# A five-layer network on one core: compression weights outside the ring, bias tables in parts, and weight rounding on two engines instead of three

## What is computed

```python
h = h + moba_nsa_mixer(rmsnorm(h), ...)      # "even": 8 heads of attention plus 8 heads that join three attentions by gates
h = h + sqrelu_mlp(rmsnorm(h), w1, w2)       # "mlp0"
h = h + fox_mixer(rmsnorm(h), ...)           # "fox": 16 heads, bias cum[q] - cum[k] from forget gates
h = h + sqrelu_mlp(rmsnorm(h), w1, w2)       # "mlp1"
x = rmsnorm(h, final_norm)
mod = silu(c) @ w_ada + b_ada                # nine vectors: shift, scale and gate three times
h = x + 0.5 * gt1 * swiglu(modulate(rmsnorm(x), sh1, sc1))      # "glu0"
h = h + gt2 * hybrid_mixer(modulate(rmsnorm(h), sh2, sc2))      # "dil": pooled channels and 8 heads
h = h + 0.5 * gt3 * swiglu(modulate(rmsnorm(h), sh3, sc3))      # "glu1"
return rmsnorm(h, g_final)
```

## Time and profile before

| | |
|---|---|
| median of 3 runs (1163.77 to 1170.25) | 1168.05 us |
| the profiled execution | 1166.54 us |
| its span, first to last instruction | 1164.7 us |
| PE, weight loads of PE | 95%, 85% |
| DVE, ACT, POOL | 66%, 48%, 11% |
| mean granted clock of PE | 0.977 |
| DMA | 236.82 MB, mean 203 GB/s |
| unit loads | 177 of 1 MB, median 5.0 us |

### The profile page before, as it was taken

One profiled execution on the slowest core, in us unless ns is written; L12 is line 12 of the kernel. 1 busy time (PEld: TensorE's weight loads), 2 busy tenths in 40 slices (PEclk: granted clock), 3 DMA queues, 4 the chain that ended last, 5 costly groups with the idle time before them and its releaser, 6 DMA issues.

```text
span 1164.7 us, 17629 instructions
## 1 busy us (share of the span) xinstructions
PE 1107.6 (95%) x7206; PEld 993.6 (85%) x7206; DVE 766.8 (66%) x1186; ACT 564.6 (48%) x843; POOL 132.2 (11%) x209
## 2 busy tenths in 40 slices
PE   6769999999999999999999999999979998999997
PEld 5768778999997988899999779999968977999996
DVE  6445666878778666676766867667676667554555
ACT  5534756434346577653433463333436767333342
POOL 2012212101001022210000110000130131000000
PEclk9779999999999999999999989999999999999999
DMA  7532326778784633486767737776754434555551
GB/s 274 222 145 73 109 97 231 276 285 292 281 287 157 249 143 109 155 296 249 244 250 253 288 144 241 267 270 253 243 193 145 145 112 162 193 186 181 181 184 70
DMA packets 39072, 236.82 MB, mean 203 GB/s; under 512 B 4389, under 2 KB 4549, under 8 KB 15952
## 3 DMA queue, kind: packets, MB, share of 16 engines
q1 hardware_dynamic: 26640, 188.76, 44.6%
q0 software_dynamic: 12064, 46.26, 11.7%
q10 hardware_dynamic: 288, 0.68, 0.2%
HBM read 234.58 MB, written 1.10 MB: 202 GB/s over the span
## 4 chain that ended last, share of the span: by engine, by line
PE 84%; DVE 7%; DMA 5%; ACT 2%; issue 1%; SPq 0%; DVEq 0%; ACTq 0%
PE bank L1389 26%; PE bank L1390 26%; PE bank L1391 26%; DMA raw<-in_stream 5%; PE bank L1579 1%; PE bank L1561 1%; PE bank L1473 1%; DVE w_lo L950 1%; PE bank L1550 1%; PE bank L1549 1%; ACT w_hi L629 1%; DVE h L981 1%; DVE w_lo L964 1%; DVE logit L1106 1%; DVE ada_raw L1168 0%
## 5 line engine op out<-in xcount | busy, mean ns | idle before, releaser
L1389 PE MATMUL bank<-a_lo,w_hi 128*128 128x256 f32 x1408 | 406.9, 289 | 6.4 <-ACT pair L851 3.3
L1390 PE MATMUL bank<-a_hi,w_lo 128*128 128x256 f32 x1408 | 402.5, 286 | 0.0
L1391 PE MATMUL bank<-a_hi,w_hi 128*128 128x256 f32 x1408 | 402.4, 286 | 0.0
L964 DVE TENSOR_TENSOR w_lo<-raw,w_hi 128x2048 fp32r<-128x2048 f32 x123 | 280.4, 2290 | 155.3 <-ACT w_hi L643 155.1
L643 ACT ACTIVATE w_hi<-raw 128x2048 fp32r<-128x2048 f32 x123 | 235.4, 1917 | 207.3 <-DMA raw<-in_stream 207.2
L1389 PEld LDWEIGHTS bank<-a_lo,w_hi 128*128 128x128 f32 x1408 | 274.4, 195 | 11.7 <-ACT pair L851 3.5
L1390 PEld LDWEIGHTS bank<-a_hi,w_lo 128*128 128x128 f32 x1408 | 274.5, 195 | 1.8
L1391 PEld LDWEIGHTS bank<-a_hi,w_hi 128*128 128x128 f32 x1408 | 274.1, 195 | 0.0
L1389 PE MATMUL bank<-w_lo,hid_hi 128*128 128x512 f32 x432 | 169.5, 392 | 0.4 <-DVE w_lo L964 0.2
L1390 PE MATMUL bank<-w_hi,hid_lo 128*128 128x512 f32 x432 | 168.9, 391 | 0.0
L1391 PE MATMUL bank<-w_hi,hid_hi 128*128 128x512 f32 x432 | 168.3, 390 | 0.0
(11 more groups left out here) (199 smaller groups left out, 1166.6 us busy)
## 6 DMA issues: line engine op xcount, KB each, us to landing
raw<-in_stream SPq DMA_DIRECT2D x177, 1024.0 KB, 5.0
ada_raw<-in_ada POOLq DMA_DIRECT2D x72, 512.0 KB, 4.8
rel_band<-rel_scratch POOLq DMA_DIRECT2D x1, 2048.0 KB, 15.4
cum_row<-cum_scratch POOLq DMA_DIRECT2D x1, 2048.0 KB, 11.1
h<-in_x SPq DMA_DIRECT2D x2, 512.0 KB, 6.6
raw<-in_stream SPq DMA_DIRECT2D x2, 512.0 KB, 7.7
silu_row<-in_c_row POOLq DMA_DIRECT2D x2, 512.0 KB, 4.3
dil_b<-in_dil_bias POOLq DMA_DIRECT2D x1, 1024.0 KB, 10.5
```

The costliest lines, as they stand in the source:

```text
L964: nc.vector.tensor_tensor(w_lo[:, u % RING, :], raw[:, u % RING, :], w_hi[:, u % RING, :].bitcast(F32), ALU.subtract).then_inc(lo_ready, 2)
L1389: nc.tensor.matmul(dst, l_hi, r_lo, start=start, stop=False)
L1390: nc.tensor.matmul(dst, l_lo, r_hi, start=False, stop=False)
L1391: return nc.tensor.matmul(dst, l_hi, r_hi, start=False, stop=stop)
```

## The change

- The four compression units leave the ring and the list of phases. They lie at the end of the stream and go into `cmpw`, two slots where the modulation rows lie later. SP issues the two of the keys behind units 3 and 5, and the two of the values in front of unit 10, behind a new wait on `cmp_used`. PE multiplies them in `compress`, in four ticks (`CMP_AT`); the later steps of that chain move to earlier ticks; the `cmp` ticks are gone and the heads' list is laid over the ticks that are left.
- `rel_band` comes in two halves, the NSA heads' behind `unit_used` 3, the others' behind 5; `cum_row` in four parts, each behind a unit; VectorE waits for each part at a tick of its own. The forget gates move one tick up. The relative-bias matmul stands behind the first turn.
- GpSimd rounds nothing. In each turn ScalarE and VectorE now round half 0 in the shifted turns too, and half 1 between block 0 and block 1.
- `ada_pieces` of `mlp1` and `glu0` end two J earlier, and the gains one J earlier.
- After the forget gates and in the dil mixer ScalarE does a one-column Exp, which loads that table early. ScalarE scales half of the output rows.

```diff
 PHASES = [
-    ("v_even", 4), ("kcvc", 1), ("kskw", 1), ("nq0", 1), ("cmp0", 1), ("nq1", 1), ("cmp1", 1), ("qm0", 1), ("cmp2", 1), ("km0", 1),
-    ("cmp3", 1), ("km1", 1), ("qm1", 1),
+    ("v_even", 4), ("kcvc", 1), ("kskw", 1), ("nq0", 1), ("nq1", 1), ("qm0", 1), ("km0", 1), ("km1", 1), ("qm1", 1),
...
-POOL_HALVES = sorted([2 * FIRST[_name] + 3 for _name in ("mlp0", "v_fox", "mlp1", "glu0", "uv_dil", "glu1")]
-                     + [2 * FIRST[_name] + 2 for _name in ("glu0", "uv_dil", "glu1")])
+CMP_UNITS = 4
...
+CMP_AT = [("nq0", 0, 1), ("nq1", 0, 0), ("qm0", 0, 0), ("qm0", 0, 1)]
 CT_AT = [("km1", 0, 1), ("km1", 0, 2), ("qm1", 0, 0), ("qm1", 0, 1)]
...
+        cmpw = place("cmpw", [P, 2, UNIT], at=V_at + 2 * D * 4)
...
-            (first, last), j0, n = ADA_OF[name], *((1, FF2 - 1) if name == "glu0" else (2, FF1 - 2))
-            return range(first + (last - first) * (j - j0) // n, first + (last - first) * (j - j0 + 1) // n)
+            (first, last), j0, n = ADA_OF[name], *{"mlp0": (2, FF1 - 2), "mlp1": (2, FF1 - 4), "glu0": (1, FF2 - 3)}[name]
+            return range(first + (last - first) * min(j - j0, n) // n, first + (last - first) * min(j - j0 + 1, n) // n)
...
             for u in range(1, N_UNITS):
                 if u >= RING:
                     sp.wait_ge(unit_used, u - RING + 1)
+                if u == FIRST["qm0"] + 2:
+                    sp.wait_ge(cmp_used, 2)
+                    for half in range(2):
+                        sp.dma_start(cmpw[:, half, :], stream[N_UNITS + 2 + half]).then_inc(cmp_landed[2 + half], 16)
                 sp.dma_start(raw[:, u % RING, :], stream[u]).then_inc(raw_landed[u % RING], 16)
+                if u in (RING - 1, RING + 1):
+                    half = (u - RING + 1) // 2
+                    sp.dma_start(cmpw[:, half, :], stream[N_UNITS + half]).then_inc(cmp_landed[half], 16)
...
-            pool.dma_start(rel_band[:, :, :], bass.AP(rel_dram, 0, [[1, P], [REL + 1, 16], [1, T]])).then_inc(rel_landed, 16)
+            pool.wait_ge(unit_used, 3)
+            pool.dma_start(rel_band[:, HEADS:16, :], bass.AP(rel_dram, HEADS * (REL + 1), [[1, P], [REL + 1, HEADS], [1, T]])).then_inc(rel_landed[0], 16)
+            pool.wait_ge(unit_used, FIRST["kskw"])
+            pool.dma_start(rel_band[:, 0:HEADS, :], bass.AP(rel_dram, 0, [[1, P], [REL + 1, HEADS], [1, T]])).then_inc(rel_landed[1], 16)
...
-            round_second("mlp0")
...
-            pool.dma_start(cum_row[:, :, :], bass.AP(cum_dram, 0, [[0, P], [T, 16], [1, T]])).then_inc(cum_landed, 16)
+            for c in range(4):
+                if c > 0:
+                    pool.wait_ge(unit_used, FIRST["qk_fox"] + c - 1)
+                pool.dma_start(cum_row[:, 4 * c:4 * c + 4, :], bass.AP(cum_dram, 4 * c * T, [[0, P], [T, 4], [1, T]])).then_inc(cum_landed[c], 16)
...
                 for t in range(TT):
                     squares(name, t)
                     if t == 0:
-                        if shift is None:
-                            round_half()
+                        round_half()
                         scale(name)
                     turned(name, t, gain, shift)
+                    if t == 0:
+                        round_half()
...
                     inverse_root(name, 0)
-                if shift is None:
-                    rest_half()
+                rest_half()
                 add(name, sums, gate, 1, 0)
                 turned(name, 0, gain, shift, (0, 1))
                 add(name, sums, gate, 1, 1)
                 turned(name, 0, gain, shift, (2, 3))
+                rest_half()
...
-                        if (name, j) == ("mlp1", FF1 - 1):
+                        if (name, j) == ("mlp1", FF1 - 2):
                             gains(("gf1", "gmix"))
...
-            nc.tensor.matmul(ps[6][0:16, 0:REL], relt[:, :], rpick[:, :], start=True, stop=True).then_inc(rel_rows, 1)
             pe.wait_ge(norms_landed, 16)
             turn_rows("mix0", 0)
+            nc.tensor.matmul(ps[6][0:16, 0:REL], relt[:, :], rpick[:, :], start=True, stop=True).then_inc(rel_rows, 1)
...
+            def compress(v, half):
+
+                pe.wait_ge(blocks_ready, v + 1)
+                pe.wait_ge(cmp_landed[2 * v + half], 16)
+                wr = cmpw[:, half, :].rearrange("p (k c) -> p k c", k=8)
+                for k in range(8):
+                    row_ = HD * (k % 2)
+                    ins = nc.tensor.matmul(ps[(2, 7)[v]][row_:row_ + 30, 0:256], blk[:, v, 8 * half + k, :], wr[:, k, :],
+                                           start=(half == 0 and k < 2), stop=(half == 1 and k >= 6))
+                ins.then_inc(cmp_used, 1)
```

More of the change, by code:

```diff
@@ L320, in build @@
         first_landed = [sem("first_landed0"), sem("first_landed1")]
+        cmp_landed = [sem(f"cmp_landed{i}") for i in range(CMP_UNITS)]
+        cmp_used = sem("cmp_used")
+        rel_landed = [sem("rel_landed0"), sem("rel_landed1")]
+        cum_landed = [sem(f"cum_landed{i}") for i in range(4)]
         hi_ready = sem("hi_ready")
@@ L727, in stack, with pairs @@
                     ins.then_inc(feat_hi, 1)
+            def pairs(v):
+                act.wait_ge(unit_used, FIRST["kcvc"] + 1)
+                for g in range(2):
+                    src = ps[4][HD * g:HD * g + HD, v * T:(v + 1) * T]
+                    nc.scalar.activation(pair[0:HD, v, g, :], src, ACT.Copy)
+                    ins = nc.scalar.activation(pair[HD:P, v, g, 0:T - 1], src[:, 1:T], ACT.Copy)
+                ins.then_inc(pairs_taken, 1)
             def values(kind, which):
@@ L844, in even_extras @@
                     values("even", (3,))
-                if tick.tag == "kskw":
-                    v = tick.part
-                    act.wait_ge(unit_used, FIRST["kcvc"] + 1)
-                    for g in range(2):
-                        src = ps[4][HD * g:HD * g + HD, v * T:(v + 1) * T]
-                        nc.scalar.activation(pair[0:HD, v, g, :], src, ACT.Copy)
-                        ins = nc.scalar.activation(pair[HD:P, v, g, 0:T - 1], src[:, 1:T], ACT.Copy)
-                    ins.then_inc(pairs_taken, 1)
-                for v, where in enumerate((("qm0", 0, 0), ("km1", 0, 0))):
+                for v, where in enumerate((("nq1", 0, 2), ("qm0", 0, 3))):
                     if tick.at(*where):
-                        act.wait_ge(unit_used, FIRST[("cmp1", "cmp3")[v]] + 1)
+                        act.wait_ge(cmp_used, 2 * v + 2)
                         nc.scalar.activation(hid_e[:, v, :], ps[(2, 7)[v]][HD:HD + 30, 0:256], ACT.Copy).then_inc(hidden_half, 1)
-                for v, where in enumerate((("qm0", 0, 2), ("km1", 0, 1))):
+                for v, where in enumerate((("qm0", 0, 0), ("km0", 0, 2))):
                     if tick.at(*where):
@@ L1247, in even_extras @@
             def even_extras(tick):
+                if tick.at("qm1", 0, 0):
+                    dve.wait_ge(rel_landed[1], 16)
                 if tick.at("kcvc", 0, 0):
@@ L1253, in even_extras @@
                     values("even", (2,))
-                if tick.at("nq1", 0, 0):
-                    dve.wait_ge(rel_landed, 16)
+                if tick.at("nq0", 0, 1):
+                    dve.wait_ge(rel_landed[0], 16)
                     nc.vector.memset(pc[:, 0:8, 7:15], BIG)
@@ L1642, in compressed_heads @@
                 ins.then_inc(cpv_done, 1)
+            def compress(v, half):
[7 more added lines that the diff above has]
+                ins.then_inc(cmp_used, 1)
             def even_extras(tick):
-                for v, where in enumerate((("qm0", 0, 2), ("km1", 0, 1))):
+                for c, where in enumerate(CMP_AT):
+                    if tick.at(*where):
+                        compress(c // 2, c % 2)
+                for v, where in enumerate((("nq1", 0, 3), ("km0", 0, 1))):
                     if tick.at(*where):
@@ L1696, in even_unit @@
                     feature_part(u, 4, part, 2)
-                elif tag.startswith("cmp"):
-                    v, half = int(tag[3]) // 2, int(tag[3]) % 2
-                    if half == 0:
-                        pe.wait_ge(blocks_ready, v + 1)
-                    wait_raw(pe, u, 1)
-                    wr = raw[:, u % RING, :].rearrange("p (k c) -> p k c", k=8)
-                    for k in range(8):
-                        row_ = HD * (k % 2)
-                        ins = nc.tensor.matmul(ps[(2, 7)[v]][row_:row_ + 30, 0:256], blk[:, v, 8 * half + k, :], wr[:, k, :],
-                                               start=(half == 0 and k < 2), stop=(half == 1 and k >= 6))
-                    ins.then_inc(unit_used, 1)
                 elif tag == "out_even":
```

113 lines of the change are left out of this document (41 added, 72 removed), and 6 rows, old and new, of the table EVEN_TICKS.

## The result

| | before | after |
|---|---|---|
| median | 1165.91 us (4 runs, 1162.93 to 1170.25) | 1125.16 us (4 runs, 1123.64 to 1126.79) |
| ratio | 1 | 0.9648, 95% interval 0.9609 to 0.9687 |
| profiled execution | 1166.54 us | 1124.25 us |
| its span | 1164.7 us | 1122.4 us |
| PE, DVE, ACT, POOL busy | 95%, 66%, 48%, 11% | 97%, 68%, 51%, 9% |

The change took off 42.3 us of the span where 31.7 were forecast.

What follows compares the result with a forecast made beforehand. TensorE, 95% busy, was taken to lose time to waits and half-clock stretches, mostly from 33 to 182 us. Gains of 25.5 + 1.9 + 3.4 + 0.9 = 31.7 us from 1166.54 gave 1134.8, set at 1135.5 us; range 1126 to 1149.

Steps and rivals of the forecast that it cites:

- The even part: Up to mlp0's first turn: 17.0 us of waits and 10.0 of half clock go, 1.5 comes back; 25.5 us gained.
- Small waits: Even part: new small waits from the moved compression work and loads, taken as 1.5 us, bounds 0 and 6.6.
- The 1.2 us for `pcT`: Even part, at 142 us: this wait stays, with its half-clock stretch costing 3.1 us.
- I leave `gf1` its half-clock stretch: First turn of gf1: its half-clock stretch, priced at 2.5 us, stays because new waits replace the old one.
- the second turns: Six turns: rounding between row blocks makes PE wait, 2.6 us in three plain turns, 6.0 in three with a shift.
- The clean-clock rival: Stretches at 142 and in gf1 go too, 3.1 + 2.5 us, if small waits do not lower the clock: 1130; chance 0.19.
- The load marks: Early loads, signs of being right: kcvc lands in 5 to 7 us, and no long `raw` load before 90 us.
- No `raw` load of more than 8 us before 90: Early loads: a sign of being right, that none before 90 us takes longer than 8 us.
- The fox part: Fox mixer: the logits' wait of 2.2 us goes, the four cum_row loads cost 0.3; 1.9 us gained.
- The turns: Turns: 11.7 us of waits and 1.5 of clock go, less 2.6 + 6.0 + 1.2; 3.4 us gained.
- The 7.9 credited to it: First turn of gmix: modulation two units ahead cuts the wait from 8.5 to some 0.6 us, 7.9 gained.
- Ends: Relative-bias matmul behind the first turn gains 0.2 us, output scalings shared with ScalarE 0.7; 0.9 gained.

Runs made afterwards that it cites:

- a_late_loads: Changed kernel with the loads of units 7 to 14 waiting until one more unit is used; span 1155.0 us.
- a_bias_whole: Changed kernel with the 2 MB bias read in one piece again, as early as in the kernel before; span 1128.9 us.
- a_mod_back: Changed kernel with the modulation's pieces and the two gains back at their old J; span 1130.0 us.
- a_cum_whole: Changed kernel with cum_row read in one 2 MB transfer again; span 1124.1 us.
- a_fox_back: Changed kernel with cum_row in one transfer and the forget gates a tick later, as before; segment mix1 to mlp1 122.11 us.
- probe1: Changed kernel with nine added waits of TensorE in glu1, made by GpSimd memsets; span 1151.5 us.
- h_plain: Changed kernel with GpSimd rounding half 1 of the second unit again in the three plain turns; median 1125.82 us.
- h_split: Changed kernel with PE's order altered in six turns, some block 0 products moved in front of the second turn; median 1124.35 us.
- b_no_pool: Kernel before with GpSimd rounding no half, ScalarE and VectorE rounding them in the turns, modulation as before; span 1157.6 us.

## Why the prediction was right and wrong

**The even part: right in place, short in size.** Forecast -25.5, measured -30.1. Waits: 17.0 - 1.5 = 15.5 forecast, 17.3 measured. Small waits (`pair`, hid, low, probT) did come, 3.3 us in all where I had left 1.5 + 0.5 + 1.0. The 1.2 us for `pcT`, which I kept "since the transposes of the compressed probabilities keep their ticks", went, and my reason looked at the wrong instructions. The transposes did keep their ticks; the last products that read `pcT` did not. Before, they stood in the same tick as the last transposes (`qm1` 0, 1), so PE waited for ScalarE's copy in between. With the heads' list laid over the new ticks they stand in a later tick (`out_even` 0, 0), some 7 us behind the copy. Before, then after:

```profile
142.17 1.12 PE L1640 MATMUL bank<-pcT,vcmp 15*64 15x256 f32 x4 [1.20 <-ACT pcT L875]
121.93 1.08 PE L1624 MATMUL bank<-pcT,vcmp 15*64 15x256 f32 x8
```

All four profiles with the old ticks have this wait with 1.20 us, and a_late_loads, with the new ticks and late engines, has none. Clock: 10.0 forecast, 12.8 measured.

**The step that failed** is "small waits, the 1.2 us for `pcT` and the half-clock stretch that comes with it at 142", with its twin "I leave `gf1` its half-clock stretch, because new waits take the place of the old one". I tied a stretch to a wait as if each wait of 1 to 2.5 us carried one. The runs show no such tie. Behind `gf1`'s second turn, with 2.50 to 2.53 us of wait each time, there was none in the changed kernel, its repeat and a_bias_whole, and one in a_mod_back, a_cum_whole, a_fox_back, a_late_loads, probe1 and h_plain. Two stretches, at 91.6 in a_bias_whole and at 88.9 in h_split, had no wait in front of them, only the sixteen narrow matmuls. In front of the one at 142, too, stood narrow matmuls beside the wait (eight products of `pcT`, on 15 partitions, from 139.89), and the clock fell at 142.09, before the wait had ended. The size was off as well: I priced `gf1`'s at 2.5, from a stretch of 6.8 us, and where it came it was 3.4 us long and cost about 1.25. In the changed kernel's profiled execution neither kept stretch came: 3.1 + 2.5 of the 10.6 us missed. Of the rest, 1.2 is `pcT`, and 2.8 are the second turns, priced at 8.6 in all and measured at 5.8; some 1.0 is left, of which 0.5 lies in front of `gf1`, where the moved modulation saves time that I hadn't counted (184.28 us in a_mod_back against 183.77).

**The clean-clock rival** (0.19) described what happened in the profiled execution. Its time, 1130, was too long because it took the waits of the forecast with it. The Trainium skill, TensorE: Matmul & The Clock Gate, section "HAM oscillation — how this bites in real kernels", has a rule by the length of the gap. The profiled execution agrees with it, but the runs above don't, with and without a stretch behind equal waits and twice with one behind no wait: by a rule on the single gap's length, both 2.85 us waits would have had the same clock. The other executions of the changed kernel, up to 2.6 us longer at clocks down to 0.996, must have had such stretches, so a clean clock is what the profiled execution had and not what the kernel always has.

**The load marks.** The kcvc load landed 4.9 us after its issue, sooner than the 5 to 7 given. "No `raw` load of more than 8 us before 90" was wrong: of the loads issued from 23 us on, three took more, 8.54 and 8.28 beside the first half of the bias, and `km1`'s 10.61 behind two loads of `cmpw`, as the prediction had it (10 us later). The first cost a wait of 1.0 at 46.6, the last none: it landed at 68.30, and PE waits nowhere from 64 to 93 us. SP's wait on `cmp_used` (10.8 us) stayed hidden, and no run shows what it costs when it doesn't. No half-clock stretch came before 90 us, and in the turns no VectorE operation on a few columns took 1 us or more; both were among the signs given for "right".

**The fox part: right.** 1.9 forecast, and the logits' wait of 2.12 us went whole. The segment with `mix1`'s 0.6 new wait in it changed by -1.8 where -1.0 was forecast; the experiments give the gain to the tick and nothing to the quarters.

**The turns.** `gmix`: forecast from 8.5 to 0.6, measured 0.33; undoing the modulation brought 4.64 back with GpSimd silent, and moving it alone took 6.9 of the 8.5. The 7.9 credited to it is thus about 4 to 7, the remainder GpSimd's hold on VectorE, and the two overlap. `gf1`: the wait went by GpSimd's silence, as I had it; a_mod_back keeps it at 0, and b_no_pool's 1.93 is a late load. The price of the second turns: plain ones 0.58 each (0.86 forecast); with a shift 2.51, 0.81 and 0.77 (2.0 each forecast). My reading, which no run isolates, is that `gf1` is the longer one since it weighs the rows and takes two roots, and that `gmix` and `gf2` have more slack than `mix1`, from which I had taken it. The delayed `a_lo`, forecast for `gmix` alone (1.2), is there with 0.90 and in `gf2` with 0.98; in `gf2` it stood before too, with 1.27.

**Ends.** -0.9 forecast, and neither part of it is seen. The second turn of the first stage, behind the relative-bias matmul's old place, began at 18.22 against 17.92. The last scalings took 0.8 us instead of 1.4, yet the kernel ended 3.9 us behind the last statistic in both. The last segment carries `gf2`'s waits as well and came out 1.2 us shorter than forecast, which is the size of the second turn's mis-sized price.

## What to carry to other kernels

A wait's name is its last link: four waits named for `w_lo`, `pair`, `probT` and the logits all ended chains through late loads, and they went when the loads were issued 11 to 33 us earlier and the bias no longer ran beside the first. Take short work out of a ring of long units, and keep big transfers from starting beside the loads that the first stages need.

When waits are removed, price the clock as a range, not as a fixed tax for each wait: with all of the kept half-clock stretches and with none. Here that difference was 5.6 us, about half of what separated forecast from result.

When a wait is expected to stay because its place is unchanged, check the places of both ends: the instruction that makes the value and the one that reads it. `pcT`'s readers had moved.

When two edits each take away a cause of one wait, try each alone, and from both kernels: in `gmix` the two gains alone (6.9 and 4.3) sum to more than both give (8.2), and in `gf1` GpSimd's silence seemed not to be enough in the kernel before, where another load was late, and was enough in the changed one.

## What the runs showed of the hardware that was not expected

- Equal waits of PE are followed by a half-clock stretch in one execution and not in another: 2.5 us in `gf1` (none in three profiled executions, one in six), 2.12 and 2.13 us for the same fox logits, 2.85 us twice in one run. Two stretches came behind no wait at all, after sixteen matmuls of 32 columns, which other runs had without one. What decides between them was not found.
- Such a stretch of 3.4 us cost 1.25 us where all else was equal (segments of 195.30 and 194.05).
- A VectorE operation on 128 x 512 took 2.61 us instead of 0.68, and one on 128 x 2 took 1.96 instead of 0.16, beside GpSimd subtractions. A price that looks like VectorE work in a profile can be another engine's.
